# Mixture-of-experts rows: weighted at PSUM and added per token in DRAM, instead of stored by place and gathered twice

## The chip, the cores and the metric

One core of one Trainium2 chip runs the whole program. The metric is the device time of one execution in microseconds (us); lower is better. Engines are called PE (TensorE), ACT (ScalarE), DVE (VectorE), POOL (GpSimd) and SP (SyncE). SP and ACT issue plain transfers on queues q1 and q10. POOL issues its transfers, indirect ones among them, on the software queue q0.

## The reference, cut to what matters

A decoder step for 1088 tokens (1024 of a prompt, 64 of samples, D = 1024): one mLSTM layer, then one MLA layer, each followed by the same kind of expert mixer. Each token goes to two of 16 experts, and the two results are added with weights that sum to one:

```python
# per layer, N = 1088 tokens, NK = 2 * N rows
se, st, sw = flat_e[order], flat_t[order], flat_w[order]      # rows sorted by expert
dest = pstarts[se] + jnp.arange(NK) - starts[se]              # each expert padded to 128-row blocks
tok_pad = jnp.full((P,), N).at[dest].set(st)
w_pad = jnp.zeros((P,)).at[dest].set(sw)
hid = silu(xb @ w_gate[e]) * (xb @ w_up[e])                   # per block of 128 rows
yb = hid @ w_down[e]
out = jnp.zeros((N + 1, D)).at[tok_pad].add(yb * w_pad[:, None])
x = layer_norm(ALPHA * x + gate2 * out[:N])                   # "combining"
```

After the first layer the combining stage also projects x to latents for the MLA layer.

## The kernel before, in words

Stages run one after another, and every stage ends in a barrier of all engines, also for its outstanding transfers. Tokens are held in nine tiles (`TILES`: eight of 128 rows, one of 64).

`stage_out_proj` (layer 0 and 1) ends with the second normalisation and the router's logits. For each tile SP stores the experts' input `h2`. In layer 0 SP also fills the last blocks of `yrows` with finite values (`L1641`, eight transfers of up to 1 MB, for the tiles 0 to 7), since unused rows of it are read later.

`stage_experts` runs once per layer. First DVE works out the routing: choices, places, tables (`choose`, `count`, `tables`, `weigh`). PE turns the places into a token number for every row of every slot (18 products of one-hot matrices, `L2149`), and POOL gathers the 128 rows of slot 0. A slot is a block of 128 rows of one expert. Layer 0 uses 26 slots and layer 1 uses 23, out of at most 32. The loops of all engines run over the slots and skip those that are not used. In a slot PE turns the gathered rows (`turn_x`, `L2074`), multiplies them with the gate and up weights (`L2082` to `L2084`, three products for each tile since every operand is split in an upper and a lower part), turns the hidden rows (`L2110`) and multiplies with the down weights into `psY`. ACT makes the upper part of the weights (`L2171`) and DVE the lower (`L2263`), only when the slot begins a new expert (`slot_fresh`; 16 of the slots of a layer). SP loads the weights of a new expert, three transfers of 2 MB, into one buffer for each of gate, up and down, so a load can start only when the part before it is split. `store(b)` on ACT copies `psY` to `y` (`L2196`) and ACT itself issues the store of `y` to `yrows` (`L2199`). The next `store` waits until that one has landed. PE's `down(b)` waits for the copy of slot b - 1. POOL's `slot(b)` waits for the gather of slot b, copies a column of token numbers (`L2059`), waits for `turn_x(b)` and gathers slot b + 1 (`L2050`).

PE's products of slot 0 stand behind `turn_x(0)` and three `keep_warm` products (`L77`), which only keep the engine busy.

`stage_combine_latents` follows layer 0. POOL gathers two rows for each token (`L2780`), with one pair of buffers ahead. ACT multiplies the first with its weight (`first`, `L2894`), DVE adds the second times its weight (`L3014`), multiplies with the gate (`L3021`) and adds the residual (`L3027`). Then come the normalisation (`L3031` on, ACT `L2906`), PE's turning (`L2809`), and the projections (`L2827` on). In the first tiles both engines also split the projection weights (`upper` on ACT, `lower` on DVE, k = 0 to 7), in an order that is written out by hand.

`stage_combine` follows layer 1 and is the last stage. POOL gathers two rows per token into `ya` and `yb`, a ring of four. ACT weights the first (`L2556`), three tiles ahead, and DVE does per tile: `both` (`L2603`), `gated` (`L2613`), `residual` (`L2618`), the mean, `centred` (`L2627`) and a reciprocal. ACT squares and makes the diagonal matrix, PE scales and adds the bias (`L2544`, `L2545`), ACT copies out and SP stores. The bias row comes through SP's loads `L2502`, `L2503`, a cast on ACT (`L2570`) and a difference on DVE (`L2637`), ahead of all else on DVE.

Of the kernel before, what the change touches and what calls it, by code (L numbers as in the profile page):

```python
# [43 lines left out]
FULL = 2 * N // P  # L44
# [1498 lines left out]
def stage_out_proj(nc, g, layer, weight, x_prompt, x_sample):  # L1543

    with nc.cleanup_on_exit(), ExitStack() as ctx:
# [58 lines left out]
        def _(sp):  # L1604
# [41 lines left out]

# [254 lines left out]
def stage_experts(nc, g, layer):  # L1901
# [6 lines left out]
    with nc.cleanup_on_exit(), ExitStack() as ctx:  # L1908
# [20 lines left out]
        tokens, tok = sb("tokens", [P, SLOTS], I32), sb("tok", [P, 1], I32)  # L1929
# [17 lines left out]
        s_split = sem("weights_all_split")  # L1947
        block = ctx.enter_context(nc.Block())
# [26 lines left out]
        hot_slot, hot_row = scratch("hot_slot", [P, 2, TILES, SLOTS], F32R), scratch("hot_row", [P, 2, TILES, P], F32R)  # L1975
# [8 lines left out]
        def table(eng, t, at):  # L1984
            most = E - 1 if t is g.slot_expert else SLOTS
            return eng.value_load(t[0:1, bass.ds(at, 1)], min_val=1 if t is g.slots_used else 0, max_val=most)
# [61 lines left out]
        def _(po):  # L2048
# [3 lines left out]

            po.wait_ge(s_tok, 1)
            gather(tokens[:, 0:1])
            po.wait_ge(s_tab, 1)

            def slot(b):
                po.wait_ge(s_x, 16 * b + 16)
                nc.gpsimd.tensor_copy(tok[:], tokens[:, bass.ds(b + 1, 1)])  # L2059
# [3 lines left out]
                gather(tok[:])  # L2063

            slots(po, slot)

        @block.tensor
        def _(pe):
# [44 lines left out]
            def down(b):  # L2113
                pe.wait_ge(s_hl, b + 1)
                pe.wait_ge(s_out, b + 1)
# [30 lines left out]
            for j, (k, lo, hi) in enumerate(((0, 0, TILES), (1, 0, 5), (1, 5, TILES))):  # L2146
                pe.wait_ge(s_row, j + 1)
                for t in range(lo, hi):
                    mm = T.matmul(psH[:, 0, 0:SLOTS], hot_row[:, k, t, :], hot_slot[:, k, t, :],  # L2149
# [4 lines left out]
            keep_warm(T, g, psG[:, 1, 0:P], 3)  # L2154
# [10 lines left out]
        def _(act):  # L2165
# [52 lines left out]
            act.sem_inc(s_st, 32)  # L2218
            act.sem_inc(s_out, 1)
# [15 lines left out]
            with act.If(used > 1):  # L2235
                slot(0, True)
            with act.Else():
                act.sem_inc(s_end, 1)
# [6 lines left out]
            with act.If(used > 1):  # L2245
                store(act.value_load(g.slots_used[0:1, 0:1], min_val=2, max_val=SLOTS) - 2)
            with act.Else():
                act.sem_inc(s_end, 1)
# [3 lines left out]
            act.wait_ge(s_st, used * 16 + 32)  # L2252
# [3 lines left out]
        def _(v):  # L2256
# [113 lines left out]
            def weigh():  # L2370
# [4 lines left out]
                for k in range(2):  # L2375
                    V.tensor_tensor(g.weight[:, k, :], g.weight[:, k, :], ws[:], ALU.mult)

            def count():
# [33 lines left out]
                for k in range(2):  # L2412
                    V.tensor_tensor(hot_slot[:, k, :, :], hot_slot[:, k, :, :].bitcast(F32), ids, ALU.mult)
# [6 lines left out]
            def tables():  # L2420
# [4 lines left out]
                V.tensor_copy(g.dest[:], destf[:])  # L2425
# [16 lines left out]
            count()  # L2442
            v.wait_ge(s_num, 1)
# [11 lines left out]
            weigh()  # L2455
            v.drain()
            lower(UP, 0)
# [10 lines left out]
def stage_combine(nc, g, layer, last):  # L2468
# [4 lines left out]
    with nc.cleanup_on_exit(), ExitStack() as ctx:  # L2473
# [3 lines left out]
        def sem(n):  # L2477
            return nc.alloc_semaphore(f"c{layer}_{n}")

        RING = 4  # L2480
# [5 lines left out]
        ya, yb = sb("ya", [P, RING, D]), sb("yb", [P, RING, D])  # L2486
# [4 lines left out]
        s_first, s_both, s_mean, s_ss, s_dev, s_cen, s_rec, s_diag, s_mm, s_x, s_st = (sem(x) for x in (  # L2491
            "first_weighted", "both_summed", "mean_ready", "squares_summed", "deviation", "centred", "reciprocal",
# [1639 lines left out]
```

## Time and profile before

| | us |
|---|---|
| runs | 2439.97, 2446.73, 2448.09 (median 2446.73) |
| profiled execution, own time | 2443.03 |
| its span, first to last instruction | 2441.4 |
| around the span | 1.6 |
| experts' stage, layer 0, first product of slot 0 to the last store | 694.7 to 1163.4 |
| experts' stage, layer 1, the same | 1951.1 to 2371.8 |
| combining with latents | 1167 to 1305 |
| last combining | 2375.5 to 2441 |

A time in a row is counted from the start of the span. The number in front of an operation in the timeline is its start, then its duration; in brackets stands the idle time of the engine before it and what ended that. Durations of matrix products overlap: in the experts' loop one starts every 0.23 us although each is listed with 0.39.

### The profile page before, as it was taken

To read this page: it belongs to the slowest core of one execution; us is meant where nothing else is said; L and a number is where in the kernel's file an instruction comes from. 1 tells how busy PE (TensorE), PEld (TensorE's weight loads), DVE (VectorE), ACT (ScalarE), POOL (GpSimd) and SP (SyncE) were. 2 spreads that over 40 slices of the span, in tenths; PEclk is the share of its full clock that TensorE was granted. 3 is DMA by queue.
4 is the path that set the end of the run, shared out by engine and by line. 5 is a ranking of instruction groups with operands and counts; after the bars stand their busy time and mean duration, and the time that the engine had idled before them with its cause. 6 is when DMAs were issued, how large, how long until landed. Compare 5 with 4: busy or idle time off the path is not lost. (4 is left out here: it accounts for less than half of the span.)

```text
span 2441.4 us, 39656 instructions
## 1 busy us (share of the span) xinstructions
PE 2260.9 (93%) x11838; PEld 1701.5 (70%) x11838; DVE 1330.0 (54%) x2251; ACT 1098.4 (45%) x1870; POOL 306.1 (13%) x387
## 2 busy tenths in 40 slices
PE   7999997889899999999798999999989899999974
PEld 4766665667688888887486565656678688888851
DVE  4222312576776756663683444433367677755757
ACT  3211212552346655663443443434343366754645
POOL 0000001670010000000100333000000011000003
PEclk8999999899999999999899999999999899999987
DMA  7566665665358767785456544333350378866846
GB/s 284 169 215 215 215 205 155 181 210 199 137 223 307 287 256 285 282 298 180 145 165 203 190 145 146 95 99 95 104 212 40 139 301 331 326 240 223 328 199 226
DMA packets 124693, 504.01 MB, mean 206 GB/s; under 512 B 19152, under 2 KB 39089, under 8 KB 105776
## 3 DMA queue, kind: packets, MB, share of 16 engines
q1 hardware_dynamic: 96270, 409.88, 47.7%
q0 software_dynamic: 18416, 64.11, 7.5%
q10 hardware_dynamic: 9906, 28.75, 3.2%
q8 instruction: 55, 0.90, 0.2%
q14 instruction: 46, 0.38, 0.0%
HBM read 437.13 MB, written 73.42 MB: 209 GB/s over the span
## 5 line engine op out<-in xcount | busy, mean ns | idle before, releaser
L2263 DVE TENSOR_TENSOR e_wl<-e_raw_gate_up,e_wh 128x1024 fp32r<-128x1024 f32 x256 | 298.5, 1221 | 88.4 <-ACT e_wh L2171 88.0
L2082 PE MATMUL e_psG<-e_wh,e_xh 128*128 128x512 f32 x784 | 315.8, 403 | 9.2 <-issue 7.6
L2084 PE MATMUL e_psG<-e_wh,e_xl 128*128 128x512 f32 x784 | 307.3, 392 | 0.0
L2083 PE MATMUL e_psG<-e_wl,e_xh 128*128 128x512 f32 x784 | 306.5, 391 | 0.0
L2171 ACT CAST e_wh<-e_raw_gate_up 128x1024 fp32r<-128x1024 f32 x256 | 251.2, 1046 | 63.9 <-DMA e_raw_gate_up<-in_e_gate 24.2
L2082 PEld LDWEIGHTS e_psG<-e_wh,e_xh 128*128 128x128 f32 x784 | 147.9, 189 | 39.0 <-issue 9.3
L2084 PEld LDWEIGHTS e_psG<-e_wh,e_xl 128*128 128x128 f32 x784 | 147.5, 188 | 32.2
L2083 PEld LDWEIGHTS e_psG<-e_wl,e_xh 128*128 128x128 f32 x784 | 148.1, 189 | 28.4
L2263 DVE TENSOR_TENSOR e_wl<-e_raw_down,e_wh 128x1024 fp32r<-128x1024 f32 x128 | 153.1, 1218 | 15.1 <-ACT e_wh L2171 15.1
L615 PE MATMUL in_ps<-in_w_upper,in_h_upper 128*128 128x512 f32 x384 | 155.3, 404 | 3.3 <-DVE in_h_lower L335 2.8
L2082 PE MATMUL e_psY<-e_wh,e_hh 128*128 128x512 f32 x392 | 154.0, 393 | 2.8 <-DVE e_hl L2286 2.8
L2084 PE MATMUL e_psY<-e_wh,e_hl 128*128 128x512 f32 x392 | 154.1, 393 | 0.0
L2083 PE MATMUL e_psY<-e_wl,e_hh 128*128 128x512 f32 x392 | 153.7, 392 | 0.0
L616 PE MATMUL in_ps<-in_w_lower,in_h_upper 128*128 128x512 f32 x384 | 150.5, 392 | 0.0
L617 PE MATMUL in_ps<-in_w_upper,in_h_lower 128*128 128x512 f32 x384 | 150.3, 391 | 0.0
L2277 DVE TENSOR_TENSOR e_xl<-e_psX,e_xh 128x512 fp32r<-128x512 f32 x98 | 67.2, 687 | 118.9 <-ACT e_xh L2182 118.9
L2171 ACT CAST e_wh<-e_raw_down 128x1024 fp32r<-128x1024 f32 x128 | 128.0, 1051 | 1.6 <-DMA e_raw_down<-in_e_down 1.6
L742 ACT ACTIVATE in_out<-in_ps 128x512 f32<-128x512 f32 (+1 forms) x54 | 32.2, 597 | 206.6 <-PE in_ps L617 202.0
L2182 ACT CAST e_xh<-e_psX 128x512 fp32r<-128x512 f32 x98 | 57.4, 588 | 149.2 <-PE e_psG L2084 124.4
L300 DVE TENSOR_TENSOR in_w_lower<-in_w_raw,in_w_upper 128x512 fp32r<-128x512 f32 x40 | 27.7, 692 | 173.2 <-ACT in_w_upper L294 172.4
L3640 ACT COPY x<-a_psP 128x512 f32<-128x512 f32 (+3 forms) x112 | 52.3, 497 | 125.9 <-PE a_psP L3487 115.9
L615 PEld LDWEIGHTS in_ps<-in_w_upper,in_h_upper 128*128 128x128 f32 x384 | 72.5, 189 | 48.1 <-ACT in_out L742 23.2
(616 smaller groups left out, 4570.9 us busy)
## 6 DMA issues: line engine op xcount, KB each, us to landing
e_raw_gate_up<-in_e_gate SPq DMA_DIRECT2D x32, 2048.0 KB, 10.0
e_raw_gate_up<-in_e_up SPq DMA_DIRECT2D x32, 2048.0 KB
e_raw_down<-in_e_down SPq DMA_DIRECT2D x32, 2048.0 KB
x<-in_ada_w SPq DMA_DIRECT2D x40, 1024.0 KB, 5.3
yrows<-e_y ACTq DMA_DIRECT2D x49, 512.0 KB, 8.7
x<-in_cache SPq DMA_DIRECT2D x64, 320.0 KB
a_pages<-in_cache SPq DMA_DIRECT2D x64, 320.0 KB, 3.5
qkvo<-in_out SPq DMA_DIRECT2D x48, 256.0 KB, 2.3
```

The source lines that it names most:

```text
L615: T.matmul(dst, up, high[:, k, :], start=(k == 0), stop=False)
L616: T.matmul(dst, up, low[:, k, :], start=False, stop=False)
L617: mm = T.matmul(dst, lw, high[:, k, :], start=False, stop=(k == KD - 1))
L742: nc.scalar.activation(out[0:n, slot, :], ps[0:n, slot, :], ACT.Sigmoid if c >= 4 else ACT.Copy).then_inc(s_ev, 1)
L2082: T.matmul(out, upper[:, k, :], wh[:, z, cols], start=k == 0, stop=False)
L2083: T.matmul(out, upper[:, k, :], wl[:, z, cols], start=False, stop=False)
L2084: mm = T.matmul(out, lower[:, k, :], wh[:, z, cols], start=False, stop=k == PIECES * n - 1)
L2171: S.copy(wh[:, z, c * PC:(c + 1) * PC], raw[z][:, c * PC:(c + 1) * PC]).then_inc(s_hi[z], 1)
L2182: S.copy(xh[:, half * 4:half * 4 + 4, :], psX[:, half * 4:half * 4 + 4, :]).then_inc(s_xh, 1)
L2263: V.tensor_tensor(wl[:, z, at], raw[z][:, at], wh[:, z, at].bitcast(F32), ALU.subtract).then_inc(s_lo[z], 1)
L2277: V.tensor_tensor(xl[at], psX[at], xh[at].bitcast(F32), ALU.subtract).then_inc(s_xl, 1)
L3640: S.copy(pT[:, par, lo:hi, :], psP[:, lo:hi, :])
```

## The change

The two rows of a token are no longer stored by place and gathered. The row's weight is multiplied in when the result leaves PSUM, and POOL adds the 128 rows of a slot to the rows of their tokens in a DRAM buffer `ysum`, by an indirect transfer that adds. Both combining stages load plain tiles of `ysum`.

- `stage_out_proj` layer 0: SP fills both layers' `ysum` with zeros, two transfers of 512 KB for each of the nine tiles, in place of the eight that filled `yrows`, and waits for all of them at the end.
- Routing: `weigh` moves ahead of the tokens' sums on DVE. A second set of 18 one-hot products, in plain f32, gives every row its weight. POOL multiplies the one-hot marks with the weights for it. The three `keep_warm` products after `turn_x(0)` go. DVE then copies `row_weight` and works out `places`, the row of `ysum` for every row of a slot (an unused row goes to a spare row).
- Loop: `store(b)` copies with a scale and issues nothing. POOL issues the adding transfer of slot b after the gather of slot b + 3, waits until it has landed, and only then goes on. ACT's next `store` waits for it.
- Combining: the gathers, ACT's `first` and DVE's weighted sum go. SP loads the first tiles at the stage's start and POOL the later ones; rings are deeper (six and four tiles).

```diff
@@ stage_out_proj, SP, per tile t
-                first = FULL + 2 * t
-                if layer == 0 and first < SLOTS:
-                    more = min(2, SLOTS - first) * P
-                    sp.dma_start(g.yrows[first * P:first * P + more, :], g.x_prompt[0:more, :]).then_inc(s_fill, 16)
+                if layer == 0:
+                    for j in range(2):
+                        sp.dma_start(g.ysum[j][t * P:(t + 1) * P, :], g.const["zeros"]).then_inc(s_fill, 16)
...
-                sp.wait_ge(s_fill, 16 * -(-(SLOTS - FULL) // 2))
+                sp.wait_ge(s_fill, 16 * 2 * TILES)
@@ stage_experts, POOL
+            def add_rows(b, landed, count):
+                nc.gpsimd.tensor_copy(tok[:, 1:2], places[:, bass.ds(b, 1)])
+                po.drain()
+                po.wait_ge(s_out, b + 4)
+                po.sem_inc(s_ask, 1)
+                nc.gpsimd.indirect_dma_start(g.ysum[layer], bass.IndirectOffsetOnAxis(tok[:, 1:2], axis=0), y[:], None,
+                                             compute_op=ALU.add).then_inc(landed, 16)
+                po.wait_ge(landed, count)
+                po.sem_inc(s_added, 1)
             po.wait_ge(s_tok, 1)
             gather(tokens[:, 0:1])
+            po.wait_ge(s_norm, 1)
+            nc.gpsimd.tensor_tensor(hot_weight[:].rearrange("p k t s -> p (k t) s"),
+                                    hot_slot[:].rearrange("p k t s -> p (k t) s"),
+                                    g.weight[:].rearrange("p k t -> p (k t)").unsqueeze(2).broadcast_to([P, 2 * TILES, SLOTS]),
+                                    ALU.mult).then_inc(s_hw, 1)
             po.wait_ge(s_tab, 1)
...
-            slots(po, slot)
+            po.wait_ge(s_rw, 1)
+            used = table(po, g.slots_used, 0)
+            slot(0)
+            slot(1)
+            with po.Fori(0, SLOTS - 3) as b:
+                with po.If(used > b + 3):
+                    slot(b + 2)
+                    add_rows(b, s_st, 16 * b + 16)
+                with po.Else():
+                    po.sem_inc(s_end, 1)
+            for j in (3, 2, 1):
+                add_rows(used - j, s_last, 64 - 16 * j)
@@ stage_experts, PE
             turn_x(0)
-            keep_warm(T, g, psG[:, 1, 0:P], 3)
+            pe.wait_ge(s_hw, 1)
+            pe.wait_ge(s_tok, 1)
+            for k in range(2):
+                for t in range(TILES):
+                    mm = T.matmul(psH[:, 1, 0:SLOTS], hot_row[:, k, t, :].bitcast(F32), hot_weight[:, k, t, :],
+                                  start=(k == 0 and t == 0), stop=(k == 1 and t == TILES - 1))
+            mm.then_inc(s_wsum, 1)
             gate(0, 0)
@@ stage_experts, ACT
             def store(b):
                 act.wait_ge(s_used[DOWN], b + 2)
-                act.wait_ge(s_st, 16 * b + 32)
+                act.wait_ge(s_added, b + 2)
                 for z in range(2):
-                    S.copy(y[:, z * HALF:(z + 1) * HALF], psY[:, z, :])
+                    S.activation(y[:, z * HALF:(z + 1) * HALF], psY[:, z, :], ACT.Copy, scale=row_weight[:, bass.ds(b, 1)])
                 act.drain()
                 act.sem_inc(s_out, 1)
-                act.dma_start(g.yrows[bass.ds(b * P, P), :], y[:]).then_inc(s_st, 16)
...
-            act.wait_ge(s_st, used * 16 + 32)
+            act.wait_ge(s_added, used + 2)
@@ stage_experts, DVE, after lower(GATE, 0, range(3, PIECES))
-            weigh()
+            v.wait_ge(s_wsum, 1)
+            V.tensor_copy(row_weight[:], psH[:, 1, 0:SLOTS])
+            V.tensor_scalar(spread[:], psH[:, 0, 0:SLOTS], 0.0, row_at[:], ALU.is_ge, ALU.mult)
             v.drain()
+            V.scalar_tensor_tensor(out=places[:], in0=psH[:, 0, 0:SLOTS], scalar=float(N), in1=spread[:],
+                                   op0=ALU.add, op1=ALU.add).then_inc(s_rw, 1)
             lower(UP, 0)
@@ stage_combine
+        def load(eng, t):
+            n, r = rows_of(t), t % RING
+            eng.dma_start(zr[0:n, r, :], g.ysum[layer][t * P:t * P + n, :]).then_inc(s_g[t], 16)
@@ SP
+            load(sp, 0)
+            load(sp, 1)
             load_mods(sp, g, gate[:, 0, :], layer, GATE2, False, s_gate)
             sp.wait_ge(s_zero, 1)
             sp.dma_start(lb33[0:1, :], g.ln_b[r:r + 1, :]).then_inc(s_lb, 16)
...
+            for t in range(2, RING):
+                load(sp, t)
@@ POOL
-            for t in range(RING, TILES):
-                po.wait_ge(s_both, t - RING + 1)
-                gather(t)
+            for t in range(RING, TILES):
+                po.wait_ge(s_cen, t - RING + 1)
+                po.wait_ge(s_ss, t - RING + 1)
+                load(po, t)
@@ DVE, per tile (ACT's first(t) goes as well)
-                V.scalar_tensor_tensor(out=z, in0=yb[0:n, r, :], scalar=g.weight[0:n, 1, t:t + 1], in1=z,
-                                       op0=ALU.mult, op1=ALU.add).then_inc(s_both, 1)
@@ stage_combine_latents, SP at the start, POOL for tiles 4 to 8
+            for i in range(4):
+                load(sp, i)
-            sp.wait_ge(s_g[0], 32)
+            sp.wait_ge(s_g[0], 16)
@@ DVE, gated(i) (ACT's first(i) goes as well)
-                V.scalar_tensor_tensor(out=z, in0=y[0:n, i % 2, 1, :], scalar=g.weight[0:n, 1, t:t + 1], in1=z,
-                                       op0=ALU.mult, op1=ALU.add)
-                v.drain()
+                v.wait_ge(s_g[i], 16)
```

## Rows read from the trace of the kernel before

**Rows 1.** The page, busy time of each engine, share of the span, instructions.

```profile
PE 2260.9 (93%) x11838; PEld 1701.5 (70%) x11838; DVE 1330.0 (54%) x2251; ACT 1098.4 (45%) x1870; POOL 306.1 (13%) x387
```

**Rows 2.** Stretches: length, busy PE, PEld, DVE, ACT, POOL, clock, DMA share, GB/s.

```profile
788.96:806.68 17.72, 17.72 (x85) 14.73 (x84) 16.30 (x17) 13.33 (x18) 2.06 (x2) 1.00 0.98 374
...
2009.84:2027.56 17.72, 17.72 (x85) 14.73 (x84) 16.29 (x16) 14.35 (x19) 3.40 (x2) 1.00 0.99 398
...
2187.04:2204.76 17.72, 17.72 (x85) 14.73 (x84) 8.58 (x10) 9.65 (x13) 1.58 (x2) 1.00 0.70 252
```

**Rows 3.** Timeline of the last combining stage.

```profile
2379.83 1.04 ACT L2570 CAST c_lb_rows<-c_lb 128x1024 fp32r<-128x1024 f32 x1 [2.34 <-DMA c_lb<-in_ln_b]
...
2394.47 1.22 DVE L2618 SCALAR_TENSOR_TENSOR c_z<-x,c_z 128x1024 f32<-128x1024 f32 x1
...
2427.39 1.22 DVE L2618 SCALAR_TENSOR_TENSOR c_z<-x,c_z 128x1024 f32<-128x1024 f32 x1
...
2432.01 0.79 PE L2544 MATMUL c_psN<-c_lb_rows,c_ones_copy 128*128 128x512 f32 x1 [2.95 <-ACT c_diagonal L2587]
```

**Rows 4.** Timeline at the end of layer 0's output projection.

```profile
659.25 0.50 SPq L1637 DMA_DIRECT2D h<-o_h  x1
...
663.61 0.35 SPq L2019 DMA_DIRECT2D e_bias<-in_router_b  x1
```

**Rows 5.** Fills of yrows (L1641), issue to landing.

```profile
DMA to landing us min/median/max: 5.0/5.9/10.8
```

**Rows 6.** Timeline of the routing in layer 0.

```profile
663.81 9.83 PE L77 MATMUL e_psG<-c_ident 128*128 128x128 f32 x72 [1.30 <-PEq L1545]
...
684.76 2.15 PE L2149 MATMUL e_psH<-e_hot_slot,e_hot_row 128*128 128x32 f32 x18 [0.23 <-DVE e_hot_row L1990]
...
693.18 0.83 PE L77 MATMUL e_psG<-c_ident 128*128 128x128 f32 x6
...
694.15 0.99 POOL L2050 DMA_INDIRECT e_xg<-h,e_tok  x1 [1.60 <-PE e_psX L2074]
...
694.74 0.50 PE L2082 MATMUL e_psG<-e_wh,e_xh 128*128 128x512 f32 x1 [0.73 <-DVE e_xl L2277]
```

**Rows 7.** Timeline inside the slot that starts at 2009.85.

```profile
2011.67 1.52 POOL L2050 DMA_INDIRECT e_xg<-h,e_tok  x1 [2.82 <-PE e_psX L2074]
...
2017.21 0.68 DVE L2282 TENSOR_TENSOR e_hid<-e_hid,e_psG 128x512 f32<-128x512 f32 x1
...
2018.91 0.60 PE L2110 MATMUL e_psH<-c_ident,e_hid 128*128 128x128 f32 x4
```

**Rows 8.** Stores of e_y by ACT (L2199), issue to landing, all 49.

```profile
DMA to landing us min/median/max: 2.6/8.7/12.4
```

**Rows 9.** Gathers L2050, issue to landing: all, then those of 1990 to 2046.

```profile
DMA to landing us min/median/max: 4.3/9.6/13.5
...
DMA to landing us min/median/max: 10.2/13.4/13.5
```

**Rows 10.** Timeline from layer 1's last store to the next stage.

```profile
2371.84 0.34 ACTq L2199 DMA_DIRECT2D yrows<-e_y  x1
2375.48 0.34 SPq L66 DMA_DIRECT2D c_gate<-mods  x1
```

**Rows 11.** Timeline of the first tiles of the combining stage with latents.

```profile
1176.36 1.28 DVE L3014 SCALAR_TENSOR_TENSOR l_y<-l_y,weight 128x1024 f32<-128x1024 f32 x1
...
1185.34 1.15 ACT L2894 ACTIVATE l_y<-l_y,weight 128x1024 f32<-128x1024 f32 x1 [7.36 <-DMA l_y<-yrows,dest]
...
1189.67 1.97 PE L2809 MATMUL l_psT<-c_ident,x 128*128 128x128 f32 x8 [7.78 <-ACT x L2906]
...
1193.41 0.64 PE L2827 MATMUL l_psK<-l_wkv_upper,l_x_upper 128*128 128x320 f32 x1 [1.77 <-DVE l_x_lower L3048]
...
1203.08 0.60 PE L2809 MATMUL l_psT<-c_ident,x 128*128 128x128 f32 x4
```

**Rows 12.** Stretches of the same stage, columns as in rows 2.

```profile
1190.00:1200.00 10.00, 8.23 (x29) 7.05 (x28) 9.23 (x16) 5.56 (x10) 1.87 (x2) 0.52 0.30 86
```

More of the change, by code:

```diff
@@ L2234, in _ @@
             used = table(act, g.slots_used, 0)
[L2235 to L2238, printed above, removed]
+            act.wait_ge(s_rw, 1)
+            slot(0, True)
             with act.Fori(1, SLOTS - 1) as b:
@@ L2244, in _ @@
             last = used - 1
[L2245 to L2248, printed above, removed]
+            store(used - 2)
             renew(DOWN, last, table(act, g.slot_fresh, last), last + 1)
@@ L2376, in weigh @@
                     V.tensor_tensor(g.weight[:, k, :], g.weight[:, k, :], ws[:], ALU.mult)
+                V.tensor_scalar(row_at[:], counts[:, P:P + 1], float(N), None, ALU.add)
+                v.drain()
+                V.memset(g.weight[NSAMP:P, :, TILES - 1:TILES], 0.0).then_inc(s_norm, 1)
             def count():
@@ L2442, in _ @@
             count()
+            weigh()
             v.wait_ge(s_num, 1)
@@ L2549, in _ @@
             S = nc.scalar
-            def first(t):
-                n, r = rows_of(t), t % RING
-                act.wait_ge(s_g[r], 32 * (t // RING) + 32)
-                if t >= RING:
-                    act.wait_ge(s_cen, t - RING + 1)
-                S.activation(zr[0:n, r, :], ya[0:n, r, :], ACT.Copy, scale=g.weight[0:n, 0, t:t + 1]).then_inc(s_first, 1)
             def out(t):
@@ L2570, in _ @@
             S.copy(both_rows[:], lb33[:]).then_inc(s_row, 1)
-            for t in range(3):
-                first(t)
             for t in range(TILES):
@@ L2649, in _ @@
                 reciprocal(t)
-                if t + 2 < TILES:
-                    both(t + 2)
             v.wait_ge(s_lbS, 16)
@@ L2776, in _ @@
         def _(po):
-            def gather(i):
-                t, n = i, rows_of(i)
-                for k in range(2):
-                    nc.gpsimd.indirect_dma_start(y[0:n, i % 2, k, :], None, g.yrows,
-                                                 bass.IndirectOffsetOnAxis(g.dest[0:n, k, t:t + 1], axis=0)
-                                                 ).then_inc(s_g[i % 2], 16)
-            gather(0)
-            po.wait_ge(s_g[0], 32)
-            gather(1)
-            for i in range(2, TILES):
-                po.wait_ge(s_mid, i - 1)
-                gather(i)
+            for i in range(4, TILES):
+                po.wait_ge(s_mid, i - 3)
+                load(po, i)
         @block.tensor
@@ L2889, in upper @@
                 act.sem_inc(s_up, 1)
-            def first(i):
-                t, n = i, rows_of(i)
-                act.wait_ge(s_g[i % 2], 32 * (i // 2) + 32)
-                S.activation(y[0:n, i % 2, 0, :], y[0:n, i % 2, 0, :], ACT.Copy,
-                             scale=g.weight[0:n, 0, t:t + 1]).then_inc(s_first, 1)
             def deviation(i):
@@ L2951, in _ @@
                 upper(k)
-            first(2)
             act.wait_ge(s_braw, KD)
@@ L3026, in middle @@
                 z = g.x[0:n, t, :]
-                V.scalar_tensor_tensor(out=z, in0=z, scalar=ALPHA, in1=y[0:n, par, 0, :], op0=ALU.mult, op1=ALU.add)
+                V.scalar_tensor_tensor(out=z, in0=z, scalar=ALPHA, in1=rows_y(i), op0=ALU.mult, op1=ALU.add)
                 v.drain()
@@ L4010, in build @@
         g.h2 = dram("h2", [N + 1, D])
-        g.yrows = dram("yrows", [SLOTS * P, D])
+        g.ysum = [dram(f"y_summed{j}", [(TILES + 1) * P, D]) for j in range(2)]
         g.x_kept = dram("x_kept", [N, D])
```

75 lines of the change are left out of this document (30 added, 45 removed).

## The prediction

> **What bounds the kernel.** I read the page first: PE is busy 93% of the span [rows 1], so a stage is worth what it moves PE, except where PE is not the bound. Next I cut both experts' stages into stretches of one slot. Every slot takes 17.72 us with PE busy throughout at clock 1.00 [rows 2]. What differs is the rest: in a slot like 2187.04 the DMA engines are 70% busy and DVE and ACT about half, but in seven slots (two of layer 0, the first at 788.96, and five of layer 1) the DMA share is 0.98 to 1.00, with DVE busy 16.3 of 17.72 us. The reader should see two things there: PE has no gap to win, and those seven slots have nothing to spare. Last come the timelines of the places where PE stands or waits: the routing, the stage ends and the two combining stages. In the last one DVE sets the pace: a residual starts every (2427.39 - 2394.47) / 6 = 5.49 us, and PE stands 2.95 before a tile [rows 3].
>
> **Zero fills, layer 0 only.** The last fill before was issued a tile ahead of the stage's end. Now two of 512 KB follow the last store of h2, issued 659.25 [rows 4], so at about 659.8 and 660.3, and the barrier waits for them. Fills took 5.0 us at least from issue to landing [rows 5], nearly all with 1 MB. 660.3 + 5.0 = 665.3, and 1.0 from the last landing to the next stage (as in layer 1: 2375.48 - 2371.84 - 2.6 [rows 8, 10]) makes 666.3 against 663.61 [rows 4]: **+2.7** (0 if they land in 2.3 us, +5 if at the median and one behind the other). The other 16 fills lie beside PE's projections; without that cover each costs SP an issue of 0.5 us.
>
> **Routing, both layers.** DVE's moved `weigh` (tiny operations and drains, about 1.1 us) falls mostly into the wait for PE's sums, +0.2. POOL's product has the time until turn_x(0), some 4 us. The new products are the term. 18 products in f32 are 36 passes. A pass of 128 columns takes 9.83 / 72 = 0.137 us; a single-pass product of 32 columns with as many weights to load takes 2.15 / 18 = 0.119 us [rows 6]. So 4.3 to 4.9 us; I take 4.6. They start when turn_x(0) ends, at 693.18 before, now 693.4. gate(0) starts at 698.0 instead of 694.74: +3.3. Copying and splitting x covers only 694.74 - 693.18 = 1.6 us of them, and that is used in this. Behind them wait `places` on DVE (0.7 us) and POOL, which has the gather of slot 1 queued behind that: issued 694.15 before [rows 6], now about 699.1, landing 4.6 later at 703.7, while PE is ready for it at 703.4; +0.4 with the wake-up. **+3.9 per layer, +7.8** (bounds +6 and +11: passes at 0.119 and no more, or at 0.137 and the gather a further 1.5 late).
>
> **Loop.** ACT's copy costs the same with a scale and loses an issue of 0.34 us; it is not the bound. In a slot that starts at T POOL gathers at T + 1.8 (2011.67 - 2009.85 [rows 7]). The copy of y is done by then or soon after, so the adding transfer starts near T + 4, and must have landed by T + 17.7 + 1.1 for ACT's next store: a limit of 14 us or a little more. No adding transfer is in the trace. From below: a plain store of the same bytes, 2.6 to 12.4, median 8.7 [rows 8]. From above: a gather, 9.6, in full slots 13.4 [rows 9], and then another behind it on the same queue, some 20 after the add's issue. I take 10 to 12 in ordinary slots, which is hidden, and 14 to 18 in the seven full ones. In those 0.5 MB more must be read, too: 0.5 / 0.39 = 1.3 us of a full DMA [rows 2]. Against that stands a slack of 2018.91 - 2017.89 = 1.0 us between DVE's product and PE's turning [rows 7]. I count 0.9 us net for each of the seven: **+6** (0 if an add costs a plain store, +25 if ACT's stores wait near 4 us in each).
>
> **End of the experts, both layers.** Before: store issued 2371.84, landed 2.6 later, next stage 2375.48 [rows 8, 10]. Now POOL wakes and issues some 0.4 later, and the add lands after 4.3 at least, if a gather in quiet is its like [rows 9]; I take 5.3. 0.4 + 5.3 - 2.6 = 3.1, say **+3.0 per layer, +6** (bounds +2 and +10 for both). The additions of the two slots before are done by then.
>
> **Combining with latents.** Tile 0 is loaded long before DVE gets to it at 1176.36; DVE's weighted sum of 1.28 goes, so mean and deviation come 1.4 us earlier. ACT stood 7.36 us for the second tile's gather and kept the deviation of tile 0 behind it [rows 11]. Without that ACT follows DVE at once, and turning starts at about 1183.9 instead of 1189.67. DVE then does one split, one gate product and the lower part of x: first projection 1186.1 instead of 1193.41. From there to turn(1) PE took 9.7 us [rows 11] for six k, at a granted clock of 0.52 until 1200 [rows 12], after standing 7.78 us. If it stays at the upper level (2.4 GHz) now, DVE's normalisation of tile 1 ends last and turn(1) starts near 1194.2, -8.9 against 1203.08. If it falls to 1.2 GHz, near 1196.6, -6.5. From there PE is busy without a gap and keeps the gain: **-7.5** (-5 to -9). Later removed operations, 2.4 us a tile over two engines, lie beside PE and give nothing.
>
> **Last combining.** Three loads of 512 KB now stand ahead of the bias row, where one and the gathers stood. It was cast 2379.83 - 2375.48 = 4.35 after SP began [rows 3, 10]; I say 6.0. From there cast, difference, gate, residual, mean, gate, centring and reciprocal take 1.04 + 1.21 + 4 x 1.24 + 0.8 = 8.0, so residual(1) starts 14.0 after SP began instead of 2394.47 - 2375.48 = 19.0: -5.0. The weighted sum goes from DVE's period: 5.49 less 1.27 is 4.22, six times: -7.6. PE had 2.95 to spare per tile [rows 3] and does not take over. **-12.6** (-10 to -15).
>
> **Sum.** +2.7 + 7.8 + 6 + 6 - 7.5 - 12.6 = +2.4. Against the profiled execution, 2443.0, that is 2445.4; the median of the runs shown is 3.7 above that execution. A measurement of this kernel can tell about 0.3% (7.3 us) from no change. I place the forecast at 2448, a little above the median.
>
> **Rivals.**
> (a) *Adds late in the full slots.* Gather and add share queue q0, and POOL stands until the add has landed; ACT's next store waits for the same, with all its weight casts behind it. For it: gathers of 13.4 us in these slots [rows 9], so an add behind one lands after T + 22. Against it: only seven slots are full. At 3 us lost in each and 1 us more in some neighbours the loop costs 16 above my 6: 2448 + 16 = 2464. It decides from 14 us of landing.
> The Trainium skill (DMA: Bandwidth & Descriptors, Queues, rings and completion order) says that each DMA engine goes round robin over the queues that have work, a packet at a time, and takes each ring in its order; by this rule, taking ACT's queue away and putting its bytes behind the gather makes the add late, which is this rival.
> (b) *Every add is slow.* Reading, adding and writing 128 rows takes 18 us in any slot: 4 us over the limit, 46 times, +184, about 2630. Nothing in the trace excludes it; the slowest store took 12.4 [rows 8].
> (c) *Adds cost no more than stores and end as fast.* Loop 0, ends +2, and a last tile at a higher clock (-1): 2443.0 + 2.7 + 7.8 + 2 - 7.5 - 13.6 = 2434. For it: stores of 2.6 in quiet [rows 8]. Against it: the software queue's 4.3 at best [rows 9]. It decides below a landing of 4 us at the ends. This one ends faster.
> (d) *Fills, routing and ends at their upper bounds* (+5, +11, +10): 2443 + 26 + 6 - 20 = 2455.
>
> **Chances.** Forecast (within 0.3%) 0.42; (c) and what lies towards it beyond 0.3%, 0.23; (a) 0.21; (b) 0.05; (d) 0.09. So faster 0.23, same 0.42, slower 0.35. The range leaves out (b) and the outer parts of (a) and (c): 2435 to 2466; the likeliest case's own is 2440 to 2454.
>
> **What would show it.** Right: twice as many transfers of POOL in the loop, adds landing in 10 to 12 us, ACT's copy waiting for them only in the full slots; gate(0) 3.3 us later after turn_x(0); first turning 17 us after the latents' stage begins instead of 22.6; residuals of the last stage every 4.2 us. Wrong: PE gaps in ordinary slots, adds over 14 us there, a fill that keeps the stage past 668, or a last stage paced by PE or by loads.

## The result: 3.3% slower, and where the profile after puts it

The changed kernel takes 2527.55 us (median of 4 runs, 2510.18 to 2538.06), the kernel before 2445.52 beside it: ratio 1.0327, 95% interval 1.0302 to 1.0353. The forecast of 2448 and its range (2435 to 2466) both miss. The profiled run took 2538.06 us, its span is 2536.4, which is 95.0 more than before.

The page of the kernel after, lines of part 1 and part 5 (busy time, mean ns of one, idle time of the engine just before, and what ended it):

```profile
PE 2293.5 (90%) x11898; PEld 1724.1 (68%) x11898; DVE 1310.8 (52%) x2241; ACT 1088.9 (43%) x1852; POOL 368.5 (15%) x459
...
L2111 PE MATMUL e_psG<-e_wh,e_xh 128*128 128x512 f32 x784 | 327.7, 418 | 71.8 <-DVE e_xl L2306 63.6
...
L2231 ACT ACTIVATE e_y<-e_psY,e_row_weight 128x512 f32<-128x512 f32 x98 | 61.9, 682 | 185.4 <-POOLq L2064 132.7
L2061 POOL DMA_INDIRECT y_summed<-e_y,e_tok x49 | 88.7, 1810 | 304.8 <-issue 269.3
```

Read from the top: PE now waits 71.8 us for x in the experts. x is late because ACT, which copies it, stood 132.7 us for L2064, POOL's word that an addition has landed. And POOL stood 269.3 us ahead of its additions for "issue", that is for nothing that the page names. That last figure is the one to follow.

The 95 us by stretch, each read from the starts of PE's turning of x (e_psX) and the stages' first instructions:

| stretch | before | after | change |
|---|---|---|---|
| start to first turning of x, layer 0 | 692.25 | 697.04 | +4.8 |
| first to second turning, layers 0 and 1 | 8.10, 8.05 | 15.29, 15.25 | +7.2, +7.2 |
| second to last turning, layer 0 (24 slots) | 425.3 | 471.1 | +45.8 |
| second to last turning, layer 1 (21 slots) | 372.4 | 401.1 | +28.7 |
| last turning to next stage, layers 0 and 1 | 41.4, 46.4 | 47.5, 62.5 | +6.1, +16.0 |
| latents' stage to first turning of layer 1 | 781.6 | 773.7 | -7.8 |
| last stage | 65.9 | 53.0 | -12.9 |

So the loss is the loop: 45.8 + 28.7, and 13.9 more in the last two slots of each layer (22.1 less the 8.2 that the ends themselves cost, below): 88 us. It is not spread evenly. Of layer 0's 24 intervals 13 still take 17.7 us and 11 take 18.5 to 26.4; in layer 1 it is 15 and 6.

One late interval of layer 1. First the stretches (length, busy PE, PEld, DVE, ACT, POOL, clock, DMA share, GB/s), then POOL, ACT and PE in the timeline:

```profile
2157.09:2174.81 17.72, 17.72 (x85) 14.73 (x84) 16.41 (x17) 14.88 (x20) 3.19 (x3) 1.00 0.97 377
2174.81:2200.76 25.95, 19.51 (x86) 15.77 (x85) 16.05 (x16) 12.11 (x16) 3.85 (x5) 0.87 0.65 201
```

```profile
2158.92 1.05 POOL L2053 DMA_INDIRECT e_xg<-h,e_tok  x1 [2.52 <-PE e_psX L2103]
2159.97 0.31 POOL L2057 COPY e_tok<-e_places 128x1 int32 x1
2171.16 1.83 POOL L2061 DMA_INDIRECT y_summed<-e_y,e_tok  x1 [10.88 <-issue]
2185.45 0.18 POOL L2077 COPY e_tok<-e_tokens 128x1 int32 x1 [12.46 <-DMA y_summed<-e_y,e_tok]
...
2184.84 1.26 ACT L2231 ACTIVATE e_y<-e_psY,e_row_weight 128x512 f32<-128x512 f32 x2 [9.00 <-POOLq L2064]
...
2187.76 0.79 PE L2111 MATMUL e_psG<-e_wh,e_xh 128*128 128x512 f32 x1 [6.44 <-DVE e_xl L2306]
```

The gather goes out at T + 1.8, as foretold. The rows of y were ready at 2159.27, the places copied at 2160.28. Yet the addition goes out at 2171.16, T + 14.1, and lands 13.4 later, at T + 27.5. ACT's store was due at T + 18.8 and comes at T + 27.75; PE loses 8.2 us. What ended POOL's 10.88 us? The gather of 2158.92 took 11.3 to land: 2170.22, and the addition follows 0.94 behind. That holds throughout: in all 43 slots of the loop the addition is issued 0.92 to 1.03 us after the gather ahead of it has landed, whether that took 4.1 or 11.3. The landings themselves (issue to landing, gathers, then additions):

```profile
DMA to landing us min/median/max: 4.1/5.4/11.3
...
DMA to landing us min/median/max: 6.0/7.8/14.4
```

Neither is slow; the gathers are faster than before [rows 9]. They are added to each other, where the prediction had them side by side. Between the gather and the addition the code has a copy and a drain on POOL. The drain stands there so that the transfer reads the number just copied (cut, with `add_rows` written out):

```python
slot(b + 2)      # wait x, copy token, drain, wait turned, gather
nc.gpsimd.tensor_copy(tok[:, 1:2], places[:, bass.ds(b, 1)])
po.drain()
po.wait_ge(s_out, b + 4)
...
nc.gpsimd.indirect_dma_start(g.ysum[layer], ...)
```

The timeline leaves drains out, but the trace has them: asked for by its line, it gives this drain (`L2058`, all 49), the same one in the late slot alone, and the drain in `slot` (`L2078`), ahead of which POOL has waited for both transfers (duration in ns, least, median, most):

```profile
L2058 POOLq DRAIN  x49: 325/5377/11448, 731.8 to 2457.9; - x49
...
L2058 POOLq DRAIN  x1: 11448/11448/11448, 2158.8 to 2158.8; - x1
...
L2078 POOLq DRAIN  x47: 326/353/1414, 706.1 to 2404.1; - x47
```

The drain of the late slot starts at 2158.82 and ends at 2170.27, with the landing of the gather. In all 43 slots of the loop `L2058` ends within 0.1 us of that landing; the addition follows 0.9 us behind the drain's end. `L2078`, with nothing in flight, takes 0.35 us in the median. So the wait is the drain's. What the runs have to show is whether it is what costs the 88 us, and whether POOL could do without it.

### The profile page after: what moved, and what is told of

The parts are those of the page before. It is cut to its first block and busy times, and to the rows that moved or that the text cites. A ratio compares the mean times of both kernels' runs of the same rounds, so it can differ in the third digit from the quotient of the medians.

```text
span 2536.4 us, 40038 instructions
## 1 busy us (share of the span) xinstructions
PE 2293.5 (90%) x11898; PEld 1724.1 (68%) x11898; DVE 1310.8 (52%) x2241; ACT 1088.9 (43%) x1852; POOL 368.5 (15%) x459
## 5 line engine op out<-in xcount | busy, mean ns | idle before, releaser
L2111 PE MATMUL e_psG<-e_wh,e_xh 128*128 128x512 f32 x784 | 327.7, 418 | 71.8 <-DVE e_xl L2306 63.6
L2113 PE MATMUL e_psG<-e_wh,e_xl 128*128 128x512 f32 x784 | 315.4, 402 | 0.0
L2112 PE MATMUL e_psG<-e_wl,e_xh 128*128 128x512 f32 x784 | 315.0, 402 | 0.0
L2111 PEld LDWEIGHTS e_psG<-e_wh,e_xh 128*128 128x128 f32 x784 | 153.4, 196 | 109.5 <-issue 80.6
L2113 PEld LDWEIGHTS e_psG<-e_wh,e_xl 128*128 128x128 f32 x784 | 152.7, 195 | 34.5
L2112 PEld LDWEIGHTS e_psG<-e_wl,e_xh 128*128 128x128 f32 x784 | 153.9, 196 | 29.3
L2231 ACT ACTIVATE e_y<-e_psY,e_row_weight 128x512 f32<-128x512 f32 x98 | 61.9, 682 | 185.4 <-POOLq L2064 132.7
L2061 POOL DMA_INDIRECT y_summed<-e_y,e_tok x49 | 88.7, 1810 | 304.8 <-issue 269.3
```

Source lines behind the costliest of these rows:

```text
L2061: nc.gpsimd.indirect_dma_start(g.ysum[layer], bass.IndirectOffsetOnAxis(tok[:, 1:2], axis=0), y[:], None, compute_op=ALU.add).then_inc(lan ...
L2111: T.matmul(out, upper[:, k, :], wh[:, z, cols], start=k == 0, stop=False)
L2112: T.matmul(out, upper[:, k, :], wl[:, z, cols], start=False, stop=False)
L2113: mm = T.matmul(out, lower[:, k, :], wh[:, z, cols], start=False, stop=k == PIECES * n - 1)
L2231: S.activation(y[:, z * HALF:(z + 1) * HALF], psY[:, z, :], ACT.Copy, scale=row_weight[:, bass.ds(b, 1)])
```

## The experiments

Theory 1: the drain waits for the gather in flight. Rival 2: POOL's indirect transfers start one at a time, drain or not. Rival 3: the addition in DRAM is itself too slow.

**e1: no drain between gather and addition.** The places are copied with the tokens, ahead of the gather.

```diff
-            def slot(b):
+            def slot(b, adds=None):
                 po.wait_ge(s_x, 16 * b + 16)
                 nc.gpsimd.tensor_copy(tok[:, 0:1], tokens[:, bass.ds(b + 1, 1)])
+                if adds is not None:
+                    nc.gpsimd.tensor_copy(tok[:, 1:2], places[:, bass.ds(adds, 1)])
                 po.drain()
...
-            def add_rows(b, landed, count):
-                nc.gpsimd.tensor_copy(tok[:, 1:2], places[:, bass.ds(b, 1)])
-                po.drain()
+            def add_rows(b, landed, count, copied=False):
+                if not copied:
+                    nc.gpsimd.tensor_copy(tok[:, 1:2], places[:, bass.ds(b, 1)])
+                    po.drain()
```

`copied` is true for the additions inside the loop, and false for the last three of a layer.

> The places of the rows to add are copied together with the tokens, ahead of the gather, so that no drain stands between the gather's issue and the addition. Theory 1 (the drain waits for the gather in flight): the addition is then issued within 2 us of the gather's issue in most slots, not 0.92 to 1.03 us after the gather's landing; the two transfers overlap, each lands later than now (gather 6 to 9, addition 9 to 14 us), most of the loop's stalls go, and the time is 2450 to 2490 us. Rival 2 (POOL's indirect transfers start one at a time whatever the program says): the addition is still issued about 1 us after the gather has landed, and the time stays at 2515 to 2535 us. Rival 3 (the addition's own cost in DRAM sets the pace): the issue moves, but its landing moves back by as much, and the time stays above 2500 us.

Measured: 2453.94 us (2452.05 to 2460.66), 1.0044 of before (1.0029 to 1.0058). One drain moved gives back 74 of the 82 us. The timeline of POOL in it, and the additions' landing:

```profile
2074.50 2.06 POOL L2053 DMA_INDIRECT e_xg<-h,e_tok  x1 [3.83 <-PE e_psX L2106]
2076.86 1.60 POOL L2062 DMA_INDIRECT y_summed<-e_y,e_tok  x1 [0.30 <-issue]
2091.11 0.18 POOL L2078 COPY e_tok<-e_tokens 128x1 int32 x1 [12.65 <-DMA y_summed<-e_y,e_tok]
...
DMA to landing us min/median/max: 6.0/9.2/18.3
```

The addition follows 0.30 us behind the gather's issue (0.95 at most, in every slot), 2.6 to 11 us ahead of its landing. Side by side both land later (gathers 7.8 in median, additions 9.2), but no longer one after the other. Layer 0's 24 intervals are 425.3 us, as before the change; layer 1 has three late ones (1.0, 2.9, 4.5). Rival 2 is out.

**e7: a bare drain put back.**

```diff
-                if not copied:
-                    nc.gpsimd.tensor_copy(tok[:, 1:2], ...)
-                    po.drain()
+                if not copied:
+                    nc.gpsimd.tensor_copy(tok[:, 1:2], ...)
+                po.drain()
```

> The kernel of e1_no_barrier (2454 us) with one bare drain put back between the gather's issue and the addition; the copy of the places stays ahead of the gather. Theory 1 (the drain is what holds POOL until the gather has landed): the addition is issued 0.9 to 1.1 us after every gather's landing again and the time is 2515 to 2535 us. If it was the copy behind the gather, and not the drain, that held it: the addition follows the gather within 1 us and the time stays at 2450 to 2460 us.

Measured: 2550.6 us in its only run, 15 us above the range expected; one run gives no interval. In its timeline:

```profile
772.83 1.00 POOL L2053 DMA_INDIRECT e_xg<-h,e_tok  x1 [2.44 <-PE e_psX L2106]
783.04 1.58 POOL L2062 DMA_INDIRECT y_summed<-e_y,e_tok  x1 [9.22 <-issue]
```

This gather landed 9.3 us after its issue, at 782.13; the addition follows 0.91 later, and in all 43 slots of the loop it is about 1.0. It is the drain alone, with nothing copied behind the gather.

**e8: the drain where it was, POOL's wait for the landing gone.** ACT's store waits for the addition directly, and two columns of places take turns (here `copied` only marks the additions inside the loop; the copy and the drain stay).

```diff
-                po.wait_ge(landed, count)
-                po.sem_inc(s_added, 1)
+                if not copied:
+                    po.wait_ge(landed, count)
+                    po.sem_inc(s_added, 1)
...
-                act.wait_ge(s_added, b + 2)
+                if landed is not None:
+                    act.wait_ge(landed, count)
```

In the loop ACT's `landed, count` are `s_st, 16 * b`.

> The changed kernel with the drain where it was, and only POOL's wait for the addition's landing taken away (ACT's store waits for it directly, as in e4_free_pool). Theory 1: the drain ahead of the next gather holds POOL until the addition has landed just the same, so nothing is won: 2515 to 2535 us, and that gather is issued about 1 us after the landing where the slot is late. Rival (the drain waits for a gather, that writes SBUF, but not for an addition, that only reads it): the next gather leaves before the addition has landed, late slots get 1 to 3 us shorter, and the time is 2480 to 2510 us.

Measured: 2531.55 us (2523.88 to 2555.2), 1.0375 (1.0324 to 1.0426). The rival of this one falls too:

```profile
2081.13 2.46 POOL L2061 DMA_INDIRECT y_summed<-e_y,e_tok  x1 [7.50 <-issue]
2083.03 1.39 POOL L2078 COPY e_tok<-e_tokens 128x1 int32 x1
2096.22 1.00 POOL L2053 DMA_INDIRECT e_xg<-h,e_tok  x1 [11.80 <-issue]
...
L2079 POOLq DRAIN  x1: 14028/14028/14028, 2081.4 to 2081.4; - x1
```

The copy runs at once, 12 us ahead of the landing (2081.13 + 14.2 = 2095.33), and the gather, which has the drain ahead of it, leaves 0.89 behind the landing. That drain (`L2079`) has a record of 14.0 us, to 2095.4. In no slot does a gather leave less than 0.84 us after the addition has landed: a drain waits for an addition as it does for a gather. POOL's explicit wait cost nothing on top of the drains.

**e4: neither.** The kernel of e1 with the edit of e8.

> As e1_no_barrier, and POOL does not wait for an addition's landing either: ACT's next store waits for it directly, which also keeps the additions in order. Theory 1: the gather leaves at T + 2 in every slot and the addition right behind it; what is left is ACT's store waiting for an addition that lands after T + 18.8, in the full slots only: 2440 to 2470 us. Rival 2: the gather of the next slot starts only when the addition has landed and the addition only when the gather has, as now: 2500 to 2535 us. Rival 3: ACT's store waits as long as now, 2500 us or more.

Measured: 2453.7 us (2444.37 to 2456.14), 1.0037 (1.0022 to 1.0052). The second to last turning takes 425.3 and 373.2 us: the loop is 0.9 us longer than before the change. Its only late interval has an addition of 16.5 us in a stretch with the DMA engines full:

```profile
2018.74:2036.46 17.72, 17.72 (x85) 14.73 (x84) 16.06 (x17) 14.77 (x19) 4.25 (x4) 1.00 1.01 389
2036.46:2055.28 18.82, 18.01 (x85) 14.65 (x84) 16.20 (x16) 13.81 (x17) 3.06 (x4) 1.00 0.90 325
```

**x3 and x8: the changed kernel and e4, overwriting and not adding.**

```diff
-  ..., y[:], None, compute_op=ALU.add).then_inc(landed, 16)
+  ..., y[:], None).then_inc(landed, 16)
```

> The same indirect transfers to the same rows with the same waits, but overwriting and not adding, so it leaves out the sum. Theory 1 and rival 2 (the order on POOL, not the addition in DRAM, is what costs): landings shorten by 1 to 2 us at most from 6.0/7.8/14.4 and the time by 10 to 40 us, to 2490 to 2520, with the issue still about 1 us behind the gather's landing. Rival 3 (the addition in DRAM is the cost): the landing falls to that of a gather, 4 to 5 us in median, and the time to 2450 to 2470 us.

> The kernel of e4_free_pool (2454 us) overwriting and not adding, so it leaves out the sum. The addition's own price once POOL stands for nothing: landings of 3.3 to 5 us instead of 6 to 9 where the queue is free, which is hidden in the loop, and about 2.7 us less at the end of each experts' stage: 2446 to 2450 us. If the additions took bandwidth or held something that the profile of e4_free_pool does not show, it falls to 2440 or below.

Measured: x3 2464.59 us (2463.61 to 2465.58), x8 2425.36 (2422.93 to 2427.0). Neither figure can be taken as it stands. Without the sums layer 1 picks other experts and has 22 slots, one less (48 indirect writes, not 49); with 17.7 us added for that slot they are about 2482.3 and 2443.1. I had not thought of that when I wrote the expectations. So read, x3 lies between the ranges of theory 1 (2490 to 2520) and rival 3 (2450 to 2470), and x8 lies 3 us under its own. The rows of x3:

```profile
L2061 POOL DMA_INDIRECT y_summed<-e_y,e_tok x48: 980/1000/1981, 736.7 to 2404.3; - x48
...
DMA to landing us min/median/max: 3.3/3.6/12.8
```

The median landing fell by 4.2 us, to 3.6, more than the 1 to 2 that I gave it and what rival 3 had foretold; each transfer still starts 1.0 us behind the gather's landing. With the drain in place the adding is worth 45 us (2527.55 - 2482.3), a little over the 10 to 40 expected: each of its 2.7 us (6.0 against 3.3 at least) goes into the chain gather, drain, addition. So rival 3 is half right: the drain strings the two transfers together, and the addition's length then decides how many slots run over: 8 intervals in x3, 17 with the adding. Overwriting, the drain still costs 39 us (2482.3 of x3 against 2443.1 of x8). Without the drain it is worth 10.6 us (2453.7 - 2443.1), of which the ends explain 5.4 (from y to the next stage 5.3 us instead of 8.0, twice). The other 5 I can't place; e4's four runs alone lie 12 us apart.

**x2: the loop undone, everything else kept.** ACT stores y to a scratch tensor as before, POOL only gathers.

> ACT stores every slot's rows as in the kernel before (to a scratch tensor that nothing reads), POOL only gathers; zero fills, weights of rows and both combining stages are the changed kernel's. It leaves out the addition, so the combining stages load zeros. By the prediction's terms for all but the loop and the ends of the experts (+2.7 + 7.8 - 7.5 - 12.6 = -9.6) it takes about 2435 us. By what the trace of the changed kernel shows of the same stages (fills +4, first interval of turning +7 per layer, latents -7.3, last stage -12.9) it takes about 2443 to 2446 us. If the changed kernel's loss lay in the fills, the weights or the combining stages, it would stay above 2480 us.

Measured: 2441.52 us (2436.2 to 2452.29, 12 runs), 0.999 (0.998 to 1.0001). All the rest of the change together wins 3.3 us (0 to 5 by the interval), where 2443 to 2446 was expected from the trace. So the loss lies in the loop and the ends. From here to e4 it is 12.2 by the medians: the two ends are 8.3 (8.0 us from y to the next stage, not 3.9) and the loop 0.4; the other 3.5 I can't place, and the profiled runs of the two lie only 5.9 apart.

**e5, e9, e10: can what is left be had?** Three moves on top of e4. The zero fills go out three at a time with the first six tiles. POOL's first two slots and ACT's first no longer wait for the row weights. The weight products are shifted against turn_x(0): in e5 nine go ahead of it and nine behind; in e9 all go ahead and DVE normalises the weights before it counts; in e10 all go ahead, but DVE's order stays. In both POOL's product of the marks moves ahead of its first gather, and the dummy products are placed anew (eight before the passes in e5, none in e9, four in e10, and three after turn_x(0) in e9 and e10).

```diff
+                if layer == 0 and t < 6:
+                    for i in range(3 * t, 3 * t + 3):
+                        sp.dma_start(g.ysum[i % 2][i // 2 * P:(i // 2 + 1) * P, :], ...)
...
-            po.wait_ge(s_rw, 1)
             slot(0)
             slot(1)
+            po.wait_ge(s_rw, 1)
```

> e4_free_pool with three moves: the 18 zero fills go out with the first six tiles; POOL's gathers of slots 1 and 2 and ACT's slot 0 no longer wait for the row weights; the first nine of the 18 weight products go ahead of turn_x(0), in place of three dummy products. Expected from the terms measured so far: -3.3 (barrier after the last h2 store back from 7.7 to 4.4 us), and per layer -1.4 for the products and 0 to -3 for the gather of slot 1: 2440 to 2447 us. The rival, that these waits are covered anyway, leaves it at 2451 to 2456 us.

> e5_placed with all 36 passes of the weight products ahead of turn_x(0): DVE normalises the weights before it takes PE's counts (about 0.8 us more on its chain), POOL multiplies the marks before its first gather, and PE's products take the place of eleven dummy ones. PE then has them done at about the time that x lands, so gate(0) starts some 4 us after turn_x(0) and not 6.4 to 7.2. Expected 2 to 3 us per layer less than e5_placed (2443.5): 2437 to 2440 us, 0.2 to 0.3% under the kernel before. Rival: the later chain of DVE and the clock that PE finds take it back: 2442 to 2445 us.

> e5_placed with POOL's product of the marks ahead of its first gather (weights normalised where they were) and all 36 passes of the weight products between the four dummy products and turn_x(0). The first gather leaves about 1.2 us later, PE is done with the passes at about the time it lands, and PE has no gap in which its clock could fall. Expected gate(0) 2 us earlier per layer than in e5_placed: about 4 us less, 2438 to 2441 us. Rival: the passes run at the lower clock as in e9_products_early and the later gather takes the rest: 2444 to 2451 us.

> The kernel of e5_placed once more, unchanged, beside e10_products_mid on the same chip: 2440 to 2447 us and a ratio of 0.997 to 1.000 if its first ratio of 0.9986 was no accident of that chip.

Measured: e5 2443.51 us (2433.0 to 2450.24, 11 runs), 0.9986 (0.9973 to 0.9999), and again 2440.81 (2433.35 to 2452.28, 12 runs), 0.9988 (0.9975 to 1.0001); e9 2451.0 (2444.43 to 2455.1), 1.0017 (1.0007 to 1.0028); e10 2444.68 (2441.11 to 2451.06), 1.0004 (0.9994 to 1.0014). The fills' move works: the next stage starts 4.7 us after the last store of h2 was issued, not 7.7. The products' move gained nothing: e9 lies above both its ranges (2437 to 2440, rival 2442 to 2445), and e10 in its rival's (2444 to 2451). The clock shows a part of why. The same passes in e9 and in the second profile of e5, and the stretch of it that holds them:

```profile
686.09 7.86 PE L2195 MATMUL e_psH<-e_hot_weight,e_hot_row 128*128 128x32 f32 x36 [0.38 <-DVE e_tokens L2487]
```

```profile
692.11 2.09 PE L2195 MATMUL e_psH<-e_hot_weight,e_hot_row 128*128 128x32 f32 x18
...
689.75:694.20 4.45, 4.45 (x41) 4.34 (x40) 4.32 (x6) 1.87 (x3) 1.46 (x2) 1.00 0.13 50
```

0.218 us a pass in e9, where the granted clock is 0.50 (686.09 to 693.76), and 0.116 at 1.00. In the first profile of e5 the clock was 0.50 in that place and the first interval 13.5 us, in the second 8.6. That is 5 us a layer that no order of mine controlled, and 10 of the 17 us between these two profiles. In e9 and e10 the passes ran at 0.50 in both layers. The first intervals of e9 are down to 9.0 and 9.5 us, but its passes, 7.9 us long, now stand ahead of turn_x(0): in layer 1 that comes 781.6 us after the latents' stage begins, in e4 773.7. e9's ratio lies 0.13% above e10's; its profile shows one late interval of 22.1 us in layer 1, but not why it should be slower in general. That stays open. No version here that adds the rows beats the kernel before by more than 0.3%.

## Why the prediction was wrong, by its own steps

**The step that failed** is in *Loop*: "The copy of y is done by then or soon after, so the adding transfer starts near T + 4". The copy of y was done by then. But I took the drain in `add_rows` for a pause of the copy's length; it holds POOL until the gather has landed (up to 11.4 us for 0.35 with nothing in flight), so the addition starts at T + 1.8 + the gather's landing (4.1 to 11.3) + 1.0, and the limit on its own landing is not 14 us but 16 less the gather's: 5 to 12. Of +6 for the loop, +88 was measured. e1 moves the drain and lands at 2453.9; e7 puts it back bare, and the loss is back. The landings that I gave the additions (10 to 12, in full slots 14 to 18) were rather too long for the changed kernel and right for e1, where they do overlap: 6.0 to 18.3. In e1 the loop costs 8.2 us by its intervals against my 6. So the sizes would have carried, and the missing wait sank it. One small premise of the same step was wrong too: ACT's copy does not cost the same with a scale, but 0.68 us on average where it was 0.59. In x2, which has the scale, the loop is 0.5 us longer in both layers together.

**The rivals.** (a) had the right place, an addition behind a gather with ACT's store after it, and the wrong mechanism (a shared queue) and price: it saw only the seven full slots, where 17 intervals and the last slots ran over. (b) named the sum of a slow addition; it was a fast one that came late. In the upper bound of the loop (+25) I had let ACT's stores wait 4 us in each full slot; no bound of mine had the two transfers in series. The Trainium skill's rule of rounds over the queues (DMA: Bandwidth & Descriptors, Queues, rings and completion order), which stood beside rival (a), does not decide here: with the same queue and the same bytes, e1 has the additions in time but for three slots.

**Zero fills** (+2.7): the stage begins 8.05 us after the last store of h2 was issued, before 4.36 [rows 4]:

```profile
660.82 0.49 SPq L1636 DMA_DIRECT2D h<-o_h  x1
661.35 1.25 SPq L1639 DMA_DIRECT2D y_summed<-const_zeros  x2
668.87 0.34 SPq L2022 DMA_DIRECT2D e_bias<-in_router_b  x1
```

+3.7, 3.3 in e1, e4 and x2. The mechanism was right, the size 1 short: the last fill landed 5.4 us after its issue and the stage follows 1.5 behind, where I had 5.0 and 1.0.

**Routing** (+3.9 a layer): +7.2 in both, outside my bounds (+6 to +11 for both together). The place was right; in this profile the size was not.

```profile
697.04 1.10 PE L2103 MATMUL e_psX<-c_ident,e_xg 128*128 128x128 f32 x8 [1.07 <-DMA e_xg<-h,e_tokens]
...
704.25 0.77 PE L2111 MATMUL e_psG<-e_wh,e_xh 128*128 128x512 f32 x1
...
697.98:704.25 6.27, 6.27 (x38) 6.27 (x37) 4.00 (x5) 2.36 (x3) 0.00 (x0) 0.61 0.01 3
704.25:709.52 5.27, 5.27 (x14) 4.11 (x15) 4.97 (x7) 0.00 (x0) 1.21 (x2) 0.50 0.10 26
```

The 36 passes took 6.3 us, not 4.6, since the granted clock was 0.61 on average over them, part at 1.2 and part at 2.4 GHz; I had priced them from rows of 0.119 and 0.137 us a pass [rows 6], and e5 shows 0.116 at clock 1.00. Then the clock stayed at 0.50 well into gate(0), where it had been 1.00 before the change: another 2.5 us. The late gather of slot 1 (+0.4) did not count here: PE has no gap before its second turning.

Where the passes found the clock at 1.00 my sum holds: in e1 the first intervals are 12.2 us in both layers, +4.1 and +4.2. But its parts were off. Here are e1's passes, and the second turning of layer 1 in x8, where the clock was 1.00 throughout and the interval 12.1:

```profile
694.50 4.10 PE L2190 MATMUL e_psH<-e_hot_weight,e_hot_row 128*128 128x32 f32 x36
...
1964.86 1.09 PE L2111 MATMUL e_psX<-c_ident,e_xg 128*128 128x128 f32 x8 [1.48 <-DMA e_xg<-h,e_tok]
```

gate(0) starts only 2.4 us later than before (4.9 us after turn_x(0) in e1 and x8, 2.5 before), not 3.3, and the gather of slot 1 keeps PE 1.5 us, not 0.4.

**Ends of the experts** (+3.0 a layer): from the end of the last copy of y to the next stage 7.8 and 8.2 us, before 3.9 in both: +3.9 and +4.3. Within the bounds; the addition needs 6.0 us at least, not 5.3, and POOL issues it 0.8 after y.

```profile
2473.98 1.26 ACT L2231 ACTIVATE e_y<-e_psY,e_row_weight 128x512 f32<-128x512 f32 x2 [8.39 <-PE e_psY L2113]
...
2476.04 1.57 POOL L2061 DMA_INDIRECT y_summed<-e_y,e_tok  x1 [17.84 <-ACTq L2232]
...
2483.40 0.81 SPq L2534 DMA_DIRECT2D c_z<-y_summed  x2
```

**Combining with latents** (-7.5): from the stage's start to turning, first projection and the second turning:

```profile
1230.93 0.30 ACT L2890 CAST l_ones<-ones 33x128 fp32r<-33x128 f32 x1 [7.81 <-PEq L1906]
...
1249.13 1.09 PE L2820 MATMUL l_psT<-c_ident,x 128*128 128x128 f32 x8 [2.09 <-ACT x L2911]
1251.56 0.42 PE L2838 MATMUL l_psK<-l_wkv_upper,l_x_upper 128*128 128x320 f32 x1 [1.34 <-DVE l_x_lower L3045]
...
1259.58 0.66 PE L2820 MATMUL l_psT<-c_ident,x 128*128 128x128 f32 x4 [0.94 <-ACT x L2911]
...
1251.56:1259.58 8.02, 7.07 (x37) 5.95 (x37) 7.30 (x15) 3.92 (x7) 0.59 (x1) 1.00 0.21 67
```

Turning starts 18.2 us into the stage, where I had 17 and before 22.6 [rows 11]; the second turning 28.65, before 36.0: -7.4, within the range. Of the two cases that I kept open it was the one at the upper level: the clock was 1.00 and from the first projection to the second turning 8.0 us passed, as I had it (8.1). That case was to give -8.9; the turning and first projection, 1.3 and 1.6 us later than I had them, take the rest back. Why they are later I did not follow up, so the nearness to -7.5 is in part luck.

**Last combining** (-12.6): the first residual after the priming tile starts 14.1 us after SP began (I had 14.0), and one follows every (2523.30 - 2497.48) / 6 = 4.30 us (I had 4.22):

```profile
2497.48 1.23 DVE L2635 SCALAR_TENSOR_TENSOR c_z<-x,c_z 128x1024 f32<-128x1024 f32 x1
...
2523.30 1.23 DVE L2635 SCALAR_TENSOR_TENSOR c_z<-x,c_z 128x1024 f32<-128x1024 f32 x1
```

The stage is 12.9 us shorter. Right.

Put together for e4, whose profiled run was its fastest (2444.37): its stretches in the order of the table above stand at +1.1, +11.1, +0.9 for both loops, +7.9, -7.8 and -12.5 to before, +0.7 in sum, which is its span of 2442.1 less 2441.4. The median of its runs lies 9 us higher; no profile of mine shows where. So freed of the drain the change about breaks even at best: what the combining stages win, the routing and the ends spend.

## What to carry to other kernels

Ask of every drain what its engine has in flight, not only which instruction it follows: on POOL, with indirect transfers in flight, it was a wait for their landing, and everything behind it was in series with them. Put the small copies that need a drain ahead of the first transfer of an iteration, so that one drain serves both. When the profile calls a long wait "issue", ask for the drains in it by their lines: their records are in the trace, though the timeline leaves them out. Then subtract the landing of the transfer in flight from the drain's end and from the next instruction's start, slot by slot, before forming a story.

## What the runs showed of the hardware

- A drain on POOL lasts until the indirect transfers that it issued have landed: its record ends within 0.1 us of a gather's landing (43 of 43 slots of the changed kernel) and of an addition's (41 of 41 in e8). The next instruction comes 0.92 to 1.03 us after a gather's landing, and never less than 0.84 us after an addition's (e8). With nothing in flight the drain takes 0.35 us (median of 47). A plain copy on POOL does not wait (2083.03 in e8).
- Two indirect transfers can be in flight from POOL: issues 0.30 us apart (e1). The gather then lands in 7.8 us and the addition in 9.2 (medians), alone 5.4 and 7.8.
- An adding transfer of 128 rows of 4 KB takes 6.0 us at least from issue to landing, overwriting the same rows 3.3; POOL spends 1.6 us on issuing it, 1.0 on the other.
- f32 passes of 32 columns with 128 by 128 weights take 0.116 us each at a granted clock of 1.00 and 0.218 at 0.50; which of the two one gets in the routing changed from profile to profile of the same kernel.
